# One inference step of a hybrid decoder on one core: another order of work in the attention rounds

## The reference

```python
s = einsum('bqhmd,bkhmd->bhmqk', q, k2) * d**-0.5      # two maps m per head
s = where(dist >= 0, s + bias, NEG_INF)
p = softmax(s)
a = p[:, :, 0] - lam * p[:, :, 1]
o = einsum('bhqk,bkhd->bqhd', a, v)                    # then per-head RMSNorm
mix = concat([o_b, o_a]) @ w_out                       # then norm, residual, ConvFFN
```

## Time and profile before

| what | value |
|---|---|
| median of 3 runs | 1360.56 us (1357.41 to 1361.14) |
| profiled execution | 1364.5 us, its span 1362.8 us |
| PE busy | 1325.5 us, 97% of the span |
| DVE, ACT, POOL busy | 730.3, 449.4, 165.4 us |
| mean granted clock of PE | 0.991 |

### The profile page before, as it was taken

One profiled execution on the slowest core, in us unless ns is written; L12 is line 12 of the kernel. 1 busy time (PEld: TensorE's weight loads), 2 busy tenths in 40 slices (PEclk: granted clock), 3 DMA queues, 4 the chain that ended last, 5 costly groups with the idle time before them and its releaser, 6 DMA issues.

```text
span 1362.8 us, 21889 instructions
## 1 busy us (share of the span) xinstructions
PE 1325.5 (97%) x8364; PEld 1195.4 (88%) x8364; DVE 730.3 (54%) x1185; ACT 449.4 (33%) x764; POOL 165.4 (12%) x323
## 2 busy tenths in 40 slices
PE   8999999988898999999999999999999999999998
PEld 7999999955665788999999989898989898989986
DVE  6447654176675564555455454546463645453555
ACT  6321001065665543352232313131323132322332
POOL 2227000021120221200000000000000000000003
PEclk9999999998998999999999999999999999999999
DMA  8576777286898242232010202020111102020117
GB/s 270 184 258 234 268 224 190 75 207 174 207 249 241 95 136 84 63 94 72 22 62 15 77 15 77 15 74 18 62 31 62 31 23 69 15 77 16 47 47 135
DMA packets 132424, 146.96 MB, mean 108 GB/s; under 512 B 25852, under 2 KB 101285, under 8 KB 132357
## 3 DMA queue, kind: packets, MB, share of 16 engines
q1 hardware_dynamic: 107865, 122.30, 30.4%
q10 hardware_dynamic: 23500, 20.24, 4.6%
q0 software_dynamic: 992, 3.54, 1.6%
HBM read 114.06 MB, written 31.47 MB: 107 GB/s over the span
## 4 chain that ended last, share of the span: by engine, by line
PE 88%; DVE 3%; DMA 2%; SPq 2%; issue 2%; ACT 1%; POOL 0%; DVEq 0%; POOLq 0%; ACTq 0%
PE PS L2500 39%; PE PS L2220 17%; PE PS L2565 16%; PE PS L2444 7%; PE PS L2580 2%; PE PS L2595 2%; PE PS L2271 1%; PE PS L2311 1%; DMA x_in<-in_x_prompt_dram 1%; DMA wo_raw<-in_w_out_dram 1%; PE PS L2374 1%; PE PS L2298 1%; PE PS L2205 1%; PE PS L2435 1%; SPq L893 1%
## 5 line engine op out<-in xcount | busy, mean ns | idle before, releaser
L2500 PE MATMUL PS<-act_lo,wu_hi 128*128 128x364 f32 (+1 forms) x1056 | 346.4, 328 | 0.0
L2500 PE MATMUL PS<-act_hi,wu_lo 128*128 128x364 f32 (+1 forms) x1056 | 346.0, 328 | 0.0
L2500 PE MATMUL PS<-act_hi,wu_hi 128*128 128x364 f32 (+1 forms) x1056 | 345.9, 328 | 0.0
L2500 PEld LDWEIGHTS PS<-act_hi,wu_hi 128*128 128x128 f32 x1056 | 198.5, 188 | 0.6
L2500 PEld LDWEIGHTS PS<-act_lo,wu_hi 128*128 128x128 f32 x1056 | 198.1, 188 | 0.4
L2500 PEld LDWEIGHTS PS<-act_hi,wu_lo 128*128 128x128 f32 x1056 | 198.4, 188 | 0.0
L1985 DVE TENSOR_TENSOR y_acc<-y_acc,PS 128x512 f32<-128x512 f32 x162 | 111.2, 687 | 116.0 <-PE PS L2565 116.0
L2565 PE MATMUL PS<-wd_hi,g_hi 128*128 128x512 f32 x324 | 130.1, 402 | 0.0
L2565 PE MATMUL PS<-wd_lo,g_hi 128*128 128x512 f32 x324 | 128.0, 395 | 0.0
L2565 PE MATMUL PS<-wd_hi,g_lo 128*128 128x512 f32 x288 | 114.0, 396 | 0.0
L1356 ACT CAST g_hi<-conv 128x1088 fp32r<-128x1088 f32 x21 | 23.2, 1105 | 245.7 <-PE PS L2565 189.7
(11 more groups left out here) (294 smaller groups left out, 2321.5 us busy)
## 6 DMA issues: line engine op xcount, KB each, us to landing
wu_raw<-in_w_up_dram SPq DMA_DIRECT2D x44, 512.0 KB, 3.9
k_tok<-in_cache_k_dram SPq DMA_DIRECT2D x64, 256.0 KB, 3.8
keys_t<-k_turned ACTq DMA_DIRECT2D x32, 512.0 KB, 4.4
vpage<-in_cache_v_dram SPq DMA_DIRECT2D x64, 256.0 KB, 4.1
wd_raw<-in_w_down_dram SPq DMA_DIRECT2D x22, 512.0 KB, 5.3
w_raw<-in_w_in_dram SPq DMA_DIRECT2D x20, 512.0 KB, 6.5
kt_mid<-keys_t SPq DMA_DIRECT2D x20, 256.0 KB, 5.9
kt_b<-keys_t SPq DMA_DIRECT2D x20, 256.0 KB, 6.3
```

The source lines that it names most:

```text
L2500: mm = nc.tensor.matmul(PS[:, 3 * half + c, 0:kept(c)], a[:, half, k, :], b[:, k, KEPT[c]], start=(j == 0), stop=(j == len(parts) - 1))
```

## The change

In words, engine by engine:

- **All:** the sample's turn moves from the rounds 6, 11, 16 to 7, 12, 17. On PE it stands behind that round's `turn` and ahead of `weigh` (before: behind `weigh`). `smp_weigh` moves one round later for the first two pairs and stays for the third.
- **DVE:** `smp_factors` is issued at the end of the round ahead of the turn, behind that round's last `mix` (before: ahead of it). In round 19 the minima of the last two steps move ahead of most splits of `w_out`, and the splits are spread between the `mix` and `out_norm` that follow.
- **ACT:** in rounds that begin with a width of 4 both exponents of that step come ahead of the copies (before: one). In rounds 2, 7, 12, 17 the first exponent comes ahead of `take_out` and `take_turned`, the second between the two `take_turned`. `smp_take` moves ahead of `take_rows`. The splits of the pieces 3, 5, 4 of `w_out` move from the rounds 17 and 18 to round 18 (piece 3) and round 19 (5 and 4, between the exponents). The list of the last round is written out anew.
- **PE:** `turn_out(6)` moves behind both `weigh` of round 19; one wait ahead of the fourth `smp_turn` is dropped.

Apart from that wait, no instruction is added or removed.

```diff
--- before.py
+++ after.py
@@ -650,8 +650,8 @@
         jobs_h = [[QB * h - 1], [0, 1], [2, 3], [4, 5], [6] if h < H - 1 else [6, 7]]
         SMP_JOBS += [[j if k == 0 else QB * h + j for j in js if k or j >= 0] for k, js in enumerate(jobs_h)]
     SMP_LAST = [RIN * (pr + 1) for pr in range(NB // 2 - 1)]
-    SMP_TURN = {s + 1: pr for pr, s in enumerate(SMP_LAST)}
-    SMP_WEIGH = {s + 2 + b2: 2 * pr + b2 for pr, s in enumerate(SMP_LAST) for b2 in range(2)}
+    SMP_TURN = {s + 2: pr for pr, s in enumerate(SMP_LAST)}
+    SMP_WEIGH = {s + 2 + (pr < NB // 2 - 2) + b2: 2 * pr + b2 for pr, s in enumerate(SMP_LAST) for b2 in range(2)}
     TURN_OUT = {ROUND_OF[subs[-1]] + 3: g for g, subs in enumerate(OUT_SETS[:6])}
 
 
@@ -1214,27 +1214,34 @@
         act.wait_ge(job_ready, len(jobs))
         for s, subs in enumerate(ROUNDS):
             before = ROUNDS[s - 1] if s >= 1 else ()
-            lead = s >= 1 and width(subs[0]) == 4
-            if lead:
-                exponent(subs[0], 0)
+            last = s == len(ROUNDS) - 1
+            if s >= 1 and width(subs[0]) == 4:
+                ahead = [(subs[0], 0), (subs[0], 1)]
+            elif s % RIN == 2:
+                ahead = [(subs[0], 0)]
+            else:
+                ahead = []
+            if last:
+                break
+            for i, m in ahead:
+                exponent(i, m)
             if s in TURN_OUT:
                 take_out(TURN_OUT[s])
-            for i in before:
-                take_turned(i)
-            if s == len(ROUNDS) - 1:
-                split_place(0, 0)
+            if s >= 1:
+                take_turned(before[0])
+            if s % RIN == 2:
+                exponent(subs[0], 1)
+                ahead.append((subs[0], 1))
+            if len(before) == 2:
+                take_turned(before[1])
             for i in SCORED[s]:
                 for m in range(2):
-                    if not (lead and i == subs[0] and m == 0):
+                    if (i, m) not in ahead:
                         exponent(i, m)
-                    if s == len(ROUNDS) - 1 and m == 0:
-                        if i == subs[0]:
-                            take_out(6)
-                        else:
-                            split_ahead(0, 1)
-            if s < len(ROUNDS) - 1:
-                if s >= 1:
-                    take_rows(before)
+            if s in SMP_TURN:
+                smp_take(SMP_TURN[s])
+            if s >= 1:
+                take_rows(before)
             if s == 1:
                 own_exponent()
             if s % RIN == 2:
@@ -1242,27 +1249,33 @@
             if s in SMP_LAST:
                 smp_exponent(s // RIN - 1, 1)
                 part_exponent(s // RIN - 1)
-            if s in SMP_TURN:
-                smp_take(SMP_TURN[s])
-            if s == len(ROUNDS) - 3:
+            if s == len(ROUNDS) - 2:
                 split_w_out(3)
-                split_w_out(5)
-            if s == len(ROUNDS) - 2:
-                split_w_out(4)
                 split_ahead(0, 0)
+        exponent(NSTEP - 2, 0)
+        take_turned(NSTEP - 4)
+        exponent(NSTEP - 2, 1)
+        take_turned(NSTEP - 3)
+        split_place(0, 0)
+        split_w_out(5)
+        exponent(NSTEP - 1, 0)
+        exponent(NSTEP - 1, 1)
+        split_w_out(4)
+        take_out(6)
+        split_ahead(0, 1)
+        take_turned(NSTEP - 2)
         split_ahead(0, 2)
+        take_rows((NSTEP - 4, NSTEP - 3))
+        split_place(0, 1)
         split_w_out(2)
-        split_place(0, 1)
-        take_turned(NSTEP - 2)
-        take_rows((NSTEP - 4, NSTEP - 3))
-        split_w_out(1)
         smp_exponent(NB // 2 - 1, 1)
         part_exponent(NB // 2 - 1)
+        take_turned(NSTEP - 1)
+        split_place(0, 2)
+        take_rows((NSTEP - 2,))
+        split_w_out(1)
         split_w_out(6)
-        split_place(0, 2)
-        take_turned(NSTEP - 1)
         split_w_out(7)
-        take_rows((NSTEP - 2,))
         take_rows((NSTEP - 1,))
         split_w_out(0)
         split_ahead(1)
@@ -1864,44 +1877,44 @@
                 out_norm(i)
             for i, m in order[3:]:
                 minima(i, m)
-            if s in SMP_TURN:
-                smp_factors(SMP_TURN[s])
             if not narrow_first(subs[0]):
                 mix(subs[0])
             if s % RIN == 2:
                 smp_softmax(s // RIN, 0)
             if len(subs) == 2:
                 mix(subs[1])
+            if s + 1 in SMP_TURN:
+                smp_factors(SMP_TURN[s + 1])
             if s == 0:
                 own_softmax()
                 own_max()
             if s in SMP_LAST:
                 smp_softmax(s // RIN - 1, 1)
         take_rows(NB - 3)
-        split_w_out(3)
-        split_w_out(5)
-        split_w_out(4)
-        split_rest(0, 0)
         minima(NSTEP - 2, 0)
         minima(NSTEP - 2, 1)
-        out_norm(NSTEP - 6)
+        split_w_out(3)
+        split_rest(0, 0)
         minima(NSTEP - 1, 0)
         minima(NSTEP - 1, 1)
+        out_norm(NSTEP - 6)
+        mix(NSTEP - 2)
+        split_w_out(5)
+        mix(NSTEP - 1)
+        smp_softmax(NB // 2 - 1, 1)
         out_norm(NSTEP - 5)
-        mix(NSTEP - 2)
-        smp_softmax(NB // 2 - 1, 1)
+        split_w_out(4)
         split_rest(0, 1)
-        mix(NSTEP - 1)
+        zero_values()
         split_rest(0, 2)
-        zero_values()
         split_w_out(2)
         out_norm(NSTEP - 4)
+        smp_factors(NB // 2 - 1)
         split_w_out(1)
-        smp_factors(NB // 2 - 1)
+        out_norm(NSTEP - 3)
         split_w_out(6)
-        out_norm(NSTEP - 3)
+        out_norm(NSTEP - 2)
         split_w_out(7)
-        out_norm(NSTEP - 2)
         split_w_out(0)
         split_rest(1)
         out_norm(NSTEP - 1)
@@ -2404,14 +2417,13 @@
                     turn(before[k])
                 if k < len(SMP_JOBS[s]):
                     smp_scores(SMP_JOBS[s][k])
+            if s in SMP_TURN:
+                smp_turn(SMP_TURN[s])
             for i in before:
                 weigh(i)
-                if i == NSTEP - 4:
-                    turn_out(6)
-            if s in SMP_TURN:
-                smp_turn(SMP_TURN[s])
             if s in SMP_WEIGH:
                 smp_weigh(SMP_WEIGH[s])
+        turn_out(6)
 
         def turn_rows(g):
             pe.wait_ge(oscaled_ready, g + 1)
@@ -2452,7 +2464,6 @@
                 pe.wait_ge(ynrm_ready, t - 1)
             for j, k in enumerate(FIRST_K if t == 0 else range(KD)):
                 if t == 0 and j == KD - 1:
-                    pe.wait_ge(onrm_ready, NSTEP - 1)
                     smp_turn(NB // 2 - 1)
                 if t == 0:
                     pe.wait_ge(wo_lo_ready, WO_SPLIT.index(k) + 1)
```

## The result

The changed kernel took 1366.62 us (median of 5 runs, 1362.49 to 1369.76) beside 1360.56 for the kernel before: a ratio of 1.005, 95% interval [1.0032, 1.0068]. It is slower by 0.5%, where 1358.4 us and no measurable change had been forecast. A second measurement gave 1370.38 us and 1.0086 [1.007, 1.0102].

What follows compares the result with a forecast made beforehand. PE was taken to bound the kernel, full behind the rounds, with gaps and low clock in them. -10.6 - 1.2 + 8.6 + 9.6 - 8.9 + 0.3 = -2.2 us, from 1360.56 to 1358.4 us; range 1354 to 1362.

Steps and rivals of the forecast that it cites:

- the removed waits: Rounds 6, 11, 16: PE's waits for `c_mat` with slow clock go, 10.6 us; gaps before rounds 10 and 15, 1.2 us.
- the new waits: Rounds 7, 12, 17: PE's turn waits 2.4, 2.4, 2.9 us for ACT's copy, plus 0.3 each: 8.6 us added.
- 16 us for the last head: Scores of round 18 to first output product: 14.0 us of PE work plus 2 us of waits.
- `w_out` and the keys, as queued: SP's queue: transfers behind later values come about the same time or some us later; ACT's first split comes at 422 or later.
- I take 3.2 us: Slow clock behind each new wait in rounds 7, 12, 17, priced like the first old wait: 9.6 us together.
- the slower rival: Rounds 7, 12, 17: half clock covers turn, weighing and next scores; decides from 5.3 us each; 1366.8 us at 6; chance 0.13.
- 16.0 us against 24.9: Last head, rounds 18 and 19: new length against the profiled old one, 8.9 us saved.
- the median of the runs is 3.9 us lower, and I take the difference over to it: Whole kernel: the profile's -2.2 us is applied to the median of 1360.56, giving 1358.4 us.
- the first output tile and what follows: First output tile: pieces of `w_out` come later in ACT's and DVE's lists, 0.3 us worse.
- The edits in the rounds 2, 5 and 10 put at nothing: ACT's exponents ahead of copies there only move work inside its list: nothing, bounds 0.7 us either way.
- the prediction has PE begin these scores when the exponent ends: Round 7's chain: PE starts scores at the exponent's end and needs 3.4 us of the 5.8 us chain, so waits 2.4.
- The third rival: Last head: `w_out` and keys land late, ACT's split stops 3 us, 5 of 8.9 us lost: 1363 us; chance 0.07.

Runs made afterwards that it cites:

- the execution of 1367.9 us: A single profiled execution of the changed kernel, no further edit, made to catch one near its median: 1367.90 us.
- before again: The kernel before, measured again without edit: 1360.72 us over 12 runs; its profiled execution took 1361.4 us.
- the new rounds alone: The changed kernel with the last head of before, except one exponent placed behind the copies in round 19: 1368.12 us, ratio 1.0065; another execution took 1362.39 us.
- the sample's turn alone: The kernel before with the sample's turn, weighing and factors moved, `smp_take` ahead of `take_rows`, and round 19's first exponent behind the copies: 1353.4 us, ratio 0.9956.
- the factors late: The changed kernel with `smp_factors` behind the first two minima of the next round: 1354.27 us, ratio 0.996.
- the exponents alone: The kernel before with only ACT's new order in the rounds (exponents ahead of copies): 1363.11 us, ratio 1.0026.
- the execution of 1360.2 us: A single profiled execution of the changed kernel, no further edit: 1360.15 us.
- copies first: The changed kernel without the exponents put ahead of `take_out` in the rounds 2, 7, 12 and 17: 1353.18 us, ratio 0.9953.
- the shorter filling: The changed kernel with unread products no longer than the waits, 9 in the rounds 7 and 12, 12 in round 17: 1358.09 us, ratio 0.999.

## Why the prediction was wrong

Set the execution of 1367.9 us, which lies between the two medians of after (1366.6 and 1370.4), against the profiled execution of before again (1361.4), which lies near that of before. The span is 6.5 us longer. By stretches, forecast and measured:

```
                                            forecast  measured
up to round 6                                  0.0      -1.5
rounds 6 to 18                                +6.4     +11.9
scores of round 18 to first output product    -8.9      -5.4
behind it                                     +0.3      +1.6
sum                                           -2.2      +6.5
```

The first line is not the change's: one and the same instruction ahead of round 1 (PE's `PS<-sk,qp`) begins at 278.4 to 280.8 us in the profiles of these kernels, and 2.1 us apart in the two of the new rounds alone. That it made the sum smaller here is chance.

**Right:** the removed waits (10.3 us by the sample's turn alone, 11.8 forecast for the waits, their slow clock and the gaps); the new waits, their length, their cause and the chain behind them (the factors late shorten them by the 1.53 us of the factors; the exponents alone give 0.63 to 0.75); that the clock can fall behind them; 16 us for the last head; that `w_out` and the keys, as queued, nearly come in time in the changed kernel (PE waits at most 1.51 us for keys, in the execution of 1360.2 us).

**The step that failed first** is "I take 3.2 us": the price of the clock behind each new wait. In an execution near the median it is 4.4, 4.5 and 4.3 us, 13.2 in place of 9.6. The argument was that no wait of 2.4 us had cost more than 3.2 in the trace of before. That trace was one execution with two such waits, in another place, where the half clock covered 7.4 us of work in the one case and 3.7 in the other; in round 7 of the execution of 1367.9 us it lasts some 10 us. The mechanism is that of the slower rival (turn, weighing and next scores at half clock), at less than the 5.3 us from which it would have decided alone. The other part of the step, half clock behind every one of the three waits, is not right of every execution: the table has one, two or three. Why the half clock lasts longer behind the new waits, no run shows. The Trainium skill (TensorE: Matmul & The Clock Gate, "Why this matters for your kernels") advises against idle gaps of TensorE above a length that lies between the two kinds of wait here. By that rule the waits of 2.47 us would cost no clock and those of 3.17 us would. The runs disagree both ways: of the twelve waits of 2.47 us in the table ten were followed by half clock, of the six of 3.17 us two.

**The second** is "16.0 us against 24.9". The new length was right, the old one was that of one execution. Near the median it is 21.7, so 5.4 us went, not 8.9. Carrying the difference over to the median, "the median of the runs is 3.9 us lower, and I take the difference over to it", counted those 3.2 us of slow clock as something the change could take away.

**Smaller terms:** the first output tile and what follows pay 1.6 us, not 0.3. The waits of 0.68 us for an exponent ahead of the scores of the rounds 7 and 12, 1.4 together, were in no term, although the prediction has PE begin these scores when the exponent ends: with the sample's turn gone from the rounds 6 and 11, PE comes to them before ACT is done. The edits in the rounds 2, 5 and 10 put at nothing come to 0.2 us up to round 6.

These account for all but some tenths: 3.6 for the clock, 1.4 for the two exponents, 3.5 for the last head, 1.3 behind it, less 1.5 ahead of round 6, are 8.3 of the 8.7 us between forecast and measurement. What stays open is why one execution has half clock behind a wait and the next does not.

The third rival, transfers too late in the last head, did not come true in the changed kernel: its waits there are at most the 1.51 us named above, in an execution whose rounds 6 to 18 took only 104.0 us. It does in each variant that has the sample's turn in its new place, goes through the rounds faster than this and keeps the old queue: waits for the keys of 4.64 us with copies first, 3.03 with the factors late and 2.37 with the shorter filling, and 11.35 us of ACT for `w_out` with the turn alone. Asking for the keys earlier took the 4.64 us away.

## What to carry to other kernels

A wait on TensorE is priced with the half clock that may follow it, and over several executions: the waits of this kernel repeat to 0.02 us while what the clock adds to them goes from 0 to 4.5 us each. When one profiled execution lies away from its median, find the stretch that makes the difference before a term is taken from that stretch. And when two edits each lengthen a chain across engines, cost them together: in the rounds 6 to 18 the turn alone brought 10.3 us and the exponents alone cost 3.1, both together cost 6.0 and 8.9, and 1.53 us of DVE's work in another place gave back 12 or more of the kernel's time. Last, when a variant is to keep a part of a kernel as it was, compare that part's rows as well: one exponent in another place took a wait of 3.5 us out of two of these variants.

## What the runs showed of the hardware that was not expected

The same program, with the same waits of 2.47, 2.47 and 3.17 us, had half clock behind one, two or three of them, and took 1359.2, 1362.5 and 1367.9 us accordingly, at a mean granted clock of 0.995, 0.993 and 0.988; the longest run took 1372.3 us at 0.986. Behind the waits of PE's turn of 0.63 to 1.63 us (the exponents alone, the factors late) these traces show none. The windows show the two ends, the stretch of round 7 in the execution of 1367.9 us (0.73) and in that of 1360.2 (1.00):

```profile
318.20:333.60 15.40, 12.64 (x74) 9.93 (x74) 8.81 (x31) 5.64 (x17) 1.57 (x3) 0.73 0.58 129
```

```profile
319.00:330.80 11.80, 8.88 (x74) 6.56 (x74) 8.74 (x30) 5.58 (x17) 1.56 (x3) 1.00 0.65 144
```

Unread products of 0.13 us a record, laid into the waits, left the clock at 1.00 through the same delay.
